# Pairs of gate columns by sums of blocks: seven block products in place of eight, and seven raw buffers

## What is computed

```python
def hybrid_layer(x, norm_w, w_in, ..., w_a_out, w_b_out, w_c_out, w_out, cos, sin, top_k):
    proj = rms_norm_2(x, norm_w) @ w_in
    (qa, ka, va, za, qi, ki, wi, ub, zb, qc, kc, vc, zc, gates) = jnp.split(proj, split_points(), axis=-1)
    ...
    y_a = (dsa_attention(qa, ka, va, qi, ki, wi, top_k) * jax.nn.silu(za)) @ w_a_out
    y_b = (conformer_conv(ub, conv_w, conv_b, cln_w, cln_b) * jax.nn.silu(zb)) @ w_b_out
    y_c = (stick_breaking_attention(qc, kc, vc) * jax.nn.silu(zc)) @ w_c_out
    g = jax.nn.sigmoid(gates).reshape(b, s, N_BRANCH, D_MODEL)
    merged = g[:, :, 0] * y_a + g[:, :, 1] * y_b + g[:, :, 2] * y_c
    return x + merged @ w_out
```

## Time and profile before

| | us |
|---|---|
| median of 3 runs (3021.7 to 3023.07) | 3022.87 |
| span of the profiled execution, first to last instruction | 3020.0 |
| PE busy in it | 3003.1 |
| ACT busy | 2288.5 |
| DVE busy | 2115.0 |

### The profile page before, as it was taken

One profiled execution on the slowest core, in us unless ns is written; L12 is line 12 of the kernel. 1 busy time (PEld: TensorE's weight loads), 2 busy tenths in 40 slices (PEclk: granted clock), 3 DMA queues, 4 the chain that ended last, 5 costly groups with the idle time before them and its releaser, 6 DMA issues.

```text
span 3020.0 us, 37810 instructions
## 1 busy us (share of the span) xinstructions
PE 3003.1 (99%) x13856; PEld 2510.0 (83%) x13856; DVE 2115.0 (70%) x3153; ACT 2288.5 (76%) x4062; POOL 7.7 (0%) x20
## 2 busy tenths in 40 slices
PE   8999999999999999999999999999999999999998
PEld 7888888878888888888888888888888888888887
DVE  6566656767666799999765555658999977555555
ACT  8799988999998677698984446786669999644564
POOL 0000000000000000000000000000000000000000
PEclk9999999999999999999999999999999999999999
DMA  8665665666556665566666666566566656666665
GB/s 307 198 175 167 180 201 174 203 181 178 178 175 199 190 192 176 172 181 181 188 184 194 190 194 196 190 198 192 162 195 180 177 172 196 187 208 192 193 191 165
DMA packets 305801, 570.24 MB, mean 189 GB/s; under 512 B 18352, under 2 KB 45136, under 8 KB 305232
## 3 DMA queue, kind: packets, MB, share of 16 engines
q1 hardware_dynamic: 301728, 557.65, 61.0%
q10 hardware_dynamic: 3040, 6.42, 0.6%
q0 software_dynamic: 848, 3.76, 0.4%
HBM read 565.66 MB, written 2.10 MB: 188 GB/s over the span
## 4 chain that ended last, share of the span: by engine, by line
PE 96%; ACT 3%; issue 0%; DMA 0%; DVE 0%; DVEq 0%; SPq 0%; ACTq 0%
PE gp L113 92%; PE bk L113 4%; ACT G L128 2%; ACT wh L128 1%; PE bk L116 0%; DMA raw<-in_ev_w_mem_kv 0%; ACT tmp L128 0%; ACT nat L128 0%; ACT Yh L128 0%; DVE wl L139 0%; DVE merged L152 0%; DVE X L139 0%; DVE merged L145 0%; DVE gp L146 0%; DVEq L2464 0%
## 5 line engine op out<-in xcount | busy, mean ns | idle before, releaser
L139 DVE TENSOR_TENSOR wl<-raw,wh 128x1024 fp32r<-128x1024 f32 (+2 forms) x1072 | 1281.3, 1201 | 723.7 <-ACT wh L128 719.8
L128 ACT ACTIVATE wh<-raw 128x1024 fp32r<-128x1024 f32 (+2 forms) x1072 | 1111.1, 1044 | 579.7 <-PE gp L113 557.9
L113 PE MATMUL gp<-wh,Hh 128*128 128x512 f32 (+2 forms) x2336 | 905.3, 388 | 0.0
L113 PE MATMUL gp<-wl,Hh 128*128 128x512 f32 (+2 forms) x2336 | 898.3, 385 | 0.0
L113 PE MATMUL gp<-wh,Hl 128*128 128x512 f32 (+2 forms) x2336 | 898.3, 385 | 0.0
L113 PE MATMUL gp<-wh,Yh 128*128 128x512 f32 (+3 forms) x1952 | 758.4, 389 | 8.8 <-DVE wl L139 8.8
L113 PE MATMUL gp<-wh,Yl 128*128 128x512 f32 (+3 forms) x1952 | 753.5, 386 | 0.0
L113 PE MATMUL gp<-wl,Yh 128*128 128x512 f32 (+3 forms) x1952 | 753.4, 386 | 0.0
L113 PEld LDWEIGHTS gp<-wh,Hh 128*128 128x128 f32 x2336 | 438.8, 188 | 87.7 <-issue 2.3
L113 PEld LDWEIGHTS gp<-wh,Hl 128*128 128x128 f32 x2336 | 438.7, 188 | 86.7
L113 PEld LDWEIGHTS gp<-wl,Hh 128*128 128x128 f32 x2336 | 438.9, 188 | 84.9
(11 more groups left out here) (135 smaller groups left out, 1196.7 us busy)
## 6 DMA issues: line engine op xcount, KB each, us to landing
raw<-in_w_in SPq DMA_DIRECT2D x544, 512.0 KB, 3.8
raw<-in_ev_w_in SPq DMA_DIRECT2D x104, 512.0 KB, 3.8
raw<-in_od_w_in SPq DMA_DIRECT2D x80, 512.0 KB, 3.7
raw<-in_w_out SPq DMA_DIRECT2D x64, 512.0 KB, 4.2
raw<-in_ev_w_out SPq DMA_DIRECT2D x40, 512.0 KB, 4.3
raw<-in_od_w_out SPq DMA_DIRECT2D x36, 512.0 KB, 4.0
raw<-in_w_b_out SPq DMA_DIRECT2D x32, 512.0 KB, 4.7
raw<-in_w_a_out SPq DMA_DIRECT2D x32, 512.0 KB, 4.9
```

The source lines that it names most:

```text
L113: return self.e.matmul(out, l, r, start=start, stop=stop)
L128: return self.e.activation(out, in_, func, **kw)
L139: return self.sketch(157 + size(a) * 1.042) if self.e is None else self.e.tensor_tensor(out, a, b, op)
```

## The change

Two neighbouring gate columns n, n + 1 of one branch are computed together, a `Duo`, where `ONLY` says so: branch 1 parts 2 and 3, all of branches 0 and 2, in both layers: ten duos. The two `y` projections follow the two gates. In a duo the eight row block pairs q are laid as two plain fills (role p, one for each column part), except q = 1, 4, 6 (`SEVEN`), where 2 x 2 blocks of the activations (A: token half x row block) and of the weights (B: row block x column part) are multiplied by Winograd's form of Strassen's scheme: seven block products. Two fills a and b are loaded. DVE forms x = (B12 - B11, B12 - B22) (`t_outer`), B22 minus the first of these in place of B12 in b (`t_inner`) and B21 - that in place of B21 in a (`t_last`); x needs a raw buffer but no transfer, y reuses a's second half. `hi` and `lo` then split all four: a, b, x of two row blocks and y of one. The matching sums of the activations are made once per layer and q by `s_sum` (five DVE operations), `s_hi`, `s_lo` into `Sh`, `Sl`, which share memory with a region of G. The products go to eight banks: both `gp` pairs and all four of the `bank` ring, which the duo takes at its first fill. Behind the duo one copy on ACT (`duo_copy`) and `duo_middle`, `duo_outer`, `duo_first`, `duo_mixed`, `duo_end` on DVE (six additions, two of them of 1024 columns) form the four results in the five `tmp` buffers, and tanh reads them from there.

Further: seven raw buffers in place of four; `half` is gone, `merge` adds 1 to the tanh, and the missing factor 0.5 moves into `in_hi` and `in_lo` of the merged values; the second `load_gfin` goes to another region of G and waits for the merged input; the memory for the descriptors of Pool's transfers is set to 4096.

```diff
-RAW = 4
+RAW = 7
 SPLIT = 4
 BY_ACT = (1,)
+SEVEN = (1, 4, 6)
+ONLY = ((1, 2), (0, 0), (0, 2), (2, 0), (2, 2))
...
-        self.raw = [sb(f"raw{i}", [128, 2, 512]) for i in range(RAW)]
+        self.raws = sb("raw", [128, 2 * RAW, 512])
+        self.raw = [self.raws[:, 2 * i:2 * i + 2, :] for i in range(RAW)]
         self.wh = [sb(f"wh{i}", [128, 2, 512], R) for i in range(SPLIT)]
         self.wl = [sb(f"wl{i}", [128, 2, 512], R) for i in range(SPLIT)]
+        with ExitStack() as early:
+            sb("ahead", [128, 1024], F, early)
+            self.Sh, self.Sl = (sb(n, [128, 4 * len(SEVEN), 128], R, early) for n in ("Sh", "Sl"))
...
+                for n in (0, 2):
+                    gates = []
+                    for m in (n, n + 1):
+                        gates.append(gemm(L, "H", 0, W, C["gates"] + 2048 * br + 512 * m, 512, 16, "gate", None, (br, m)))
+                        if (br, n) not in ONLY:
+                            merge[br, m] = (gates[-1], gemm(L, "Y", lo, I[name][l], 512 * m, 512, 8, "y", None, (br, m)))
+                    if (br, n) in ONLY:
+                        duo(*gates)
+                        for m in (n, n + 1):
+                            merge[br, m] = (gates[m - n], gemm(L, "Y", lo, I[name][l], 512 * m, 512, 8, "y", None, (br, m)))
             self.merge.append(merge)
-            self.h_end[L] = gate
+            self.h_end[L] = gates[1]
...
+    def lay_duo(self, d):
+        for q in range(d.a.nk // 2):
+            for role, gm in (zip("abxy", (d.a, d.b, d.b, d.b)) if q in SEVEN else (("p", d.a), ("p", d.b))):
+                f = len(self.fills)
+                self.role[f] = (role, d, q)
+                self.fills.append((gm, q))
+                d.units.append(f)
+                for bank, _, kk, t in self.parts(f):
+                    d.first.setdefault(bank, (f, kk, t))
+                    d.last[bank] = (f, kk, t)
+        d.a.end = d.b.end = f
+
+    def parts(self, f):
+
+        role, d, q = self.role[f]
+        gm, i = self.fills[f][0], 4 * SEVEN.index(q) if q in SEVEN else 0
+        if role == "p":
+            names = ("11", "21") if gm is d.a else ("12", "22")
+            return [(names[t], (kk, t), kk, t) for kk in range(2) for t in range(2)]
+        return {"a": [("1", (0, 0), 0, 0), ("11", (1, 0), 1, 0)], "b": [("6", i + 2, 0, 0), ("12", i + 3, 1, 0)],
+                "x": [("5", i, 0, 0), ("7", i + 1, 1, 0)], "y": [("21", (1, 1), 1, 0)]}[role]
...
+    def place_raw(self):
+
+        self.slot, self.leaves, self.loaded_before = [], [], []
+        holder, n, loaded = [None] * RAW, 0, None
+        for f in range(len(self.fills)):
+            role = self.role[f][0] if f in self.role else None
+            self.loaded_before.append(loaded)
+            if role not in ("x", "y"):
+                loaded = f
+            if role == "y":
+                self.slot.append(self.slot[f - 3])
+                self.leaves.append(None)
+                continue
+            self.slot.append(n % RAW)
+            self.leaves.append(holder[n % RAW])
+            holder[n % RAW] = f + 3 if role == "a" else f
+            n += 1
...
+    def banks_of(self, d):
+        g, h = self.gp[d.a.g % 2], self.gp[d.b.g % 2]
+        return {"1": g[:, 0, :], "11": g[:, 1, :], "6": h[:, 0, :], "22": h[:, 1, :], "12": self.four[:, 0, :],
+                "21": self.four[:, 1, :], "5": self.four[:, 2, :], "7": self.four[:, 3, :]}
...
+            n = gm.duo.n
+            return self.v_duo.at(*(((n, "v1"), (n, "c11")) if gm is gm.duo.a else ((n, "v1"), (n, "c22"))))
...
-        if f < RAW:
+        if f < 4:
             e.behind("load_memt", f)
         else:
-            e.behind("raw", f - 1)
-            e.wait_ge(*P.v_lo.at(f - RAW))
-        if f == RAW:
+            e.behind("raw", P.loaded_before[f])
+        if f == 4:
             e.behind("load_memt", 4)
+        if P.leaves[f] is not None:
+            e.wait_ge(*P.v_lo.at(P.leaves[f]))
...
+        e.wait_ge(*P.v_in.at(*([("m", 1, i) for i in range(0, 16, 2)] if f else [("y", 9, 2)])))
+        e.dma_start(P.gfin[f], g.unsqueeze(0).broadcast_to([128, 2048])).then_inc(*P.s_gfin[f].up("g", 16))
...
+        if f == d.units[0]:
+            for i in range(4):
+                P.bank.take(("duo", d.n, i))
+        e.wait_ge(*P.v_lo.at(f))
+        if f == d.units[0]:
+            e.wait_ge(*P.drained(P.gemms[d.a.g - 2]))
+            for i in range(4):
+                e.wait_ge(*P.bank.free(("duo", d.n, i)))
+        if f == d.units[1]:
+            e.wait_ge(*P.drained(P.gemms[d.b.g - 2]))
+        if role in ("b", "x"):
+            e.wait_ge(*P.v_s.at((P.lhs(gm, 2 * q)[0:2], q)))
+        bk = P.banks_of(d)
+        lh, ll = P.pairs[gm.side][gm.L]
+        for bank, of, kk, t in P.parts(f):
+            if role in ("b", "x"):
+                h, l = P.Sh[:, of, :], P.Sl[:, of, :]
+            else:
+                k, c = 2 * q + of[0], slice(128 * of[1], 128 * of[1] + 128)
+                e.wait_ge(*ready(gm, k))
+                h, l = lh[:, gm.lo + k, c], ll[:, gm.lo + k, c]
+            wh, wl = P.wh[s][:, kk, :], P.wl[s][:, kk, :]
+            e.matmul(bk[bank], h, wh, d.first[bank] == (f, kk, t), False)
+            e.matmul(bk[bank], h, wl, False, False)
+            i = e.matmul(bk[bank], l, wh, False, d.last[bank] == (f, kk, t))
+        i.then_inc(*P.p_mm.up(f))
...
+        role = P.role[f][0] if f in P.role else None
+        if role in ("b", "x", "y"):
+            e.wait_ge(*P.v_tsum.at((f - "abxy".index(role), {"b": 2, "x": 1, "y": 4}[role])))
+        if role not in ("x", "y"):
+            e.wait_ge(*P.raw_loaded(f))
...
+    def t_outer(f):
+
+        a, b, x = (P.slot[f + i] for i in range(3))
+        e.wait_ge(*P.raw_loaded(f))
+        e.wait_ge(*P.raw_loaded(f + 1))
+        if P.leaves[f + 2] is not None:
+            e.wait_ge(*P.v_lo.at(P.leaves[f + 2]))
+        i, j = 2 * a, 2 * b + 1
+        s = slice(i, j + 1, j - i) if i < j else slice(i, j - 1 if j else None, j - i)
+        b12 = P.raw[b][:, 0, :].unsqueeze(1).broadcast_to([128, 2, 512])
+        e.tensor_tensor(P.raw[x], b12, P.raws[:, s, :], ALU.subtract).then_inc(*P.v_tsum.up((f, 1)))
+
+    def t_inner(f):
+        a, b, x = (P.raw[P.slot[f + i]] for i in range(3))
+        e.wait_ge(*P.v_tsum.at((f, 1)))
+        e.tensor_tensor(b[:, 0, :], b[:, 1, :], x[:, 0, :], ALU.subtract).then_inc(*P.v_tsum.up((f, 2)))
+
+    def t_last(f):
+        a, b = (P.raw[P.slot[f + i]] for i in range(2))
+        e.wait_ge(*P.v_tsum.at((f, 2)))
+        e.wait_ge(*P.v_lo.at(f))
+        e.tensor_tensor(a[:, 1, :], a[:, 1, :], b[:, 0, :], ALU.subtract).then_inc(*P.v_tsum.up((f, 4)))
...
+        e.tensor_tensor(a, h, lo[:, at:at + 2, :].bitcast(F), ALU.add).then_inc(*P.v_ssum.up((*key, "a")))
+        e.wait_ge(*P.v_ssum.at((*key, "a")))
+        e.tensor_tensor(s[:, 0, :], a[:, 0, 128:256], a[:, 1, 128:256], ALU.add).then_inc(*P.v_ssum.up((*key, 1)))
+        e.tensor_tensor(s[:, 1, :], a[:, 0, 128:256], a[:, 0, 0:128], ALU.subtract).then_inc(*P.v_ssum.up((*key, 3)))
+        e.wait_ge(*P.v_ssum.at((*key, 1)))
+        e.tensor_tensor(s[:, 2, :], s[:, 0, :], a[:, 0, 0:128], ALU.subtract).then_inc(*P.v_ssum.up((*key, 2)))
+        e.wait_ge(*P.v_ssum.at((*key, 2)))
+        e.tensor_tensor(s[:, 3, :], a[:, 1, 0:128], s[:, 2, :], ALU.subtract).then_inc(*P.v_ssum.up((*key, 4)))
...
+        e.tensor_tensor(T[:, 1, :], P.banks_of(d)["6"], T[:, 0, :], ALU.add).then_inc(*v.up((n, "v1")))
...
+        one = T[:, 1, :].unsqueeze(1).broadcast_to([128, 2, 512])
+        e.tensor_tensor(T[:, 2:4, :], one, P.four[:, 2:4, :], ALU.add).then_inc(*v.up((n, "v2")))
+        e.wait_ge(*v.at((n, "v2")))
+        e.tensor_tensor(T[:, 4, :], T[:, 3, :], P.four[:, 2, :], ALU.add).then_inc(*v.up((n, "c22 begun")))
...
+        e.tensor_tensor(T[:, 0, :], P.banks_of(d)["11"], T[:, 0, :], ALU.add).then_inc(*v.up((n, "c11")))
...
+        e.tensor_tensor(T[:, 2:4, :], T[:, 2:4, :], P.four[:, 0:2, :], ALU.add).then_inc(*v.up((n, "c12")))
...
+        e.tensor_tensor(T[:, 4, :], P.banks_of(d)["22"], T[:, 4, :], ALU.add).then_inc(*v.up((n, "c22")))
...
-    def half(g):
-        b = P.nat.buf(g)
-        e.wait_ge(*P.a_evac.at((g, "end")))
-        e.tensor_scalar(b, b, 0.5, 0.5, ALU.mult, ALU.add).then_inc(*P.v_half.up(g))
...
-            e.tensor_tensor(m, ps[:, :, :], b, ALU.mult).then_inc(*P.v_m.up((g, 0)))
+            e.scalar_tensor_tensor(m, b, 1.0, ps[:, :, :], ALU.add, ALU.mult).then_inc(*P.v_m.up((g, 0)))
...
-        if s.name in ("hi", "lo"):
+        if s.name in ("hi", "lo", "t_outer", "t_inner", "t_last"):
             return 0 if s.args[0] - plan.at_fill <= 3 else 4
-        if s.name == "evac":
+        if s.name == "evac" or s.name[0:3] == "duo":
...
-    nc = _bacc.Bacc("TRN2", target_bir_lowering=False, num_devices=1)
+    nc = _bacc.Bacc("TRN2", target_bir_lowering=False, num_devices=1, dynamic_dma_scratch_size=4096)
```

(52 more changed lines are left out.)

183 lines of the change are left out of this document (148 added, 35 removed).

## The result

| | before | changed |
|---|---|---|
| median of 5 runs, us | 3022.92 | 3002.35 |
| lowest to highest | 3021.7 to 3023.1 | 3001.31 to 3002.67 |
| span of the profiled execution | 3020.0 | 3000.9 |

The ratio is 0.9933, with a 95% interval of 0.9921 to 0.9945: 20.57 us faster. The forecast was 3005.5 us in a range of 3000.5 to 3017, or 3002 to 3010 without rival 1. The kernel before has two runs more here than in the table before the change, so its median moved by 0.05 us.

A forecast was written before the change was run, and what follows sets the result against it. The prediction took PE's own matmul issue to bound the kernel: 3022.87 - 20.4 for removed matmuls + 3 for stalls = 3005.5 us, in a range of 3000.5 to 3017, or 3002 to 3010 as the forecast's own case.

The forecast's parts named there:

- rival 1: In the duos: stalls take 0.2 to 0.6 us from each pair, giving 3014.5 us (3010 to 3016.8); chance 0.16.
- What bounds the kernel: In both merge stages PE is busy every microsecond, so its own issue sets the time, 0.2267 us per matmul.
- 90 matmuls x 0.2267 = 20.4 us: On PE: 30 pairs take 21 matmuls in place of 24, saving 20.4 us in all.
- 2.87 us around the span: Outside the profiled execution: the median of 3022.87 us exceeds the 3020.0 us span by 2.87 us, carried over unchanged.
- Stalls, 0.3 us per duo: PE's waits in the ten duos: 3 us in all, chosen between zero and 19 us.
- hand-run order: DVE's operations from pair 4 to pair 6, timed: they fit with one to three microseconds to spare.
- That needs the seventh raw buffer: DVE running ahead in the pairs needs seven raw buffers, as x occupies one and a stays until y's lo.
- Quarter 2 has 7 us of slack: Before the output projection: quarter 2's flip and 16 moves need 12 us, leaving 7 us of slack.
- half at nothing: Removing half from DVE (24 x 0.694 us) gains nothing, as that engine had idle time; 16.7 us if DVE bound.
- Rival 3: In the pairs DVE becomes the bound, each costing 6.9 us in place of 4.76: 3068 us; chance 0.10.
- Rival 4: Short waits in the duos lower the granted clock and 143 us of pairs would double: 3145 us; chance 0.01.
- The start: At program start, three more transfers of 512 KB go out: value 0, bounds -1 to +2.5 us.

The follow-up runs named there:

- no_duo: The changed kernel with no duo at all, gate columns one by one, all other edits kept; 3022.13 us, ratio 0.9997 to the kernel before.
- raw5: The changed kernel with five raw buffers in place of seven; 3008.31 us, 6.0 us slower than with seven.
- raw6: The changed kernel with six raw buffers in place of seven; 3002.38 us, the same as seven.
- one_pair: The changed kernel with ten duos but only row block pair 4 taking seven products, 10 such pairs in place of 30; 3015.02 us.
- half_back: The changed kernel with the half step back on DVE and the old merge, in_hi and in_lo; 3003.47 us.
- adjacent_pairs: The changed kernel with its seven-product pairs next to each other, 3, 4, 5 in place of 1, 4, 6; 3035.0 us.
- first_gates_b: The changed kernel with two duos more, at each layer's first gates, and the four small banks handed back together at a duo's end; 3029.22 us.
- out_duo: The changed kernel with one duo more, in the first two column parts of the last layer's output projection; 3007.08 us.

## Why the prediction was right, step by step

**What bounds the kernel**: right. Nothing but matmul starts sets the time in the merge stages; no_duo shows that the other edits together are worth zero within 1 us.

**90 matmuls x 0.2267 = 20.4 us**: right. Measured 20.57 between medians. The two profiled executions differ by 19.1 us, and the difference can be followed: the two stretches of duos are 10.1 and 9.8 us shorter, the rest 0.1, and the first duo begins 0.9 us later (1579.59 for 1578.66). The last comes from the start of the program. Both run a first stretch of matmuls 0.43 us apart behind the wait of the start; it is longer in the profiled execution of the changed kernel. The last matmul that starts 0.43 us after the one ahead of it, before and after:

```profile
11.96 0.41 PE L113 MATMUL gp<-wl,Yh 128*128 128x512 f32 x1
```
```profile
14.24 0.52 PE L115 MATMUL gp<-wl,Yh 128*128 128x512 f32 x1
```

They lie 3.2 and 5.7 us behind the first matmul (8.81 and 8.52). The spacing beyond 0.2267 adds up to 1.6 us before and 2.9 after, and the first matmul is 0.3 earlier: 1.0 us. The same excess is 1.8 us in no_duo, 1.9 in raw5, 2.1 in raw6 and 2.7 in one_pair. Among these raw5, raw6 and one_pair differ from the changed kernel only in what comes much later or in a buffer, so I put the difference down to the execution and not to the change; no run settles it. It fits that the profiled execution of the changed kernel has the longest span of its five runs (2999.5 to 3000.9).

**2.87 us around the span**: wrong. Where time and span of a run are both on record, they differ by 1.75 to 1.92 us in all but a few. The 2.87 compared the median with the span of one execution, a short one. The forecast starts from the median, so nothing came of it.

**Stalls, 0.3 us per duo**: the term that was mis-sized. It was 3 us and measured 0.5: the two stretches fall short of 10.2 us each by 0.1 and 0.4. The largest gap is 0.2 us near 2868, and two of 0.1 stand at the second fill of each layer's first duo. That is 2.5 of the 3.1 us by which the forecast missed; the rest is less than the runs scatter. The 3 us was a choice between 0 and 19 that no row gave, so that the number came this near is in part luck, and 3002.35 lies at the very edge of the narrower range of 3002 to 3010. The hand-run order was right in the main. Counted from a of pair 4, which starts at 1600.77 on PE, the rows under raw5 and raw6 give for seven buffers: `lo` of y at 0.9 (foretold 0.98), `t_outer` 1.7 (1.7), `t_inner` 5.2 (4.2), `t_last` 7.1 (8.6), `lo` of b and x done at 10.1 (10.4), `lo` of y at 11.1 (11.1). Only `t_inner` and `t_last` stand elsewhere, 1.0 later and 1.5 earlier than foretold. I had added something for collisions, and as I read it the list planner, which sees each of them, had already arranged them away; no run without it shows that.

**"That needs the seventh raw buffer"**: wrong. raw6 is as fast. Six suffice for the lead; with five it costs 6.0 us. The lead of `t_outer` over b's matmul is what counts: 9.8 us with seven buffers, about 6 with six, and a block without slack with five.

**Quarter 2 has 7 us of slack**: wrong, 1.7 us. I let the flip follow the merge at once and let nothing follow the moves. In the program the first `merge` operation ends at 1886.43, the flip starts 3.8 us later, the 16 moves between `hi`s take 9.0 (1891.67 to 1900.68), and `in_lo` follows only 3.7 after them: 18.7 us in place of 12. half_back shows what stands behind it.

**half at nothing**: right for DVE's time, wrong in that the end of the merge stage was nearer than I had it. The rows named for the new `merge` hold no scalar_tensor_tensor; in the changed kernel it takes 1.22 us at 1024 columns, as assumed (1885.21).

**Rival 3, DVE becomes the bound**: not in this kernel, but real two steps away. Its price was 2.2 us for each pair; adjacent_pairs loses 1.1 us per pair, lower clock included, because in each duo the combinations of the first two pairs are still made ahead, in whole or in part, and PE waits about 2 us in the third alone. **Rival 4, the clock**: cycling through eight banks does not lower it: granted 1.00 in both stretches. The kernel before went round four already, two pairs in turn. The Trainium skill, "TensorE: Matmul & The Clock Gate", section "A second HAM failure mode: psum-queue depth-cycling", tells of an engine that idles for short times between its groups of matmuls while it cycles through banks. A duo has no such pause between its groups, so this case neither confirms nor refutes the page. Where the clock did fall (adjacent_pairs, first_gates_b, out_duo) it fell behind a wait, and the price behind one in adjacent_pairs and out_duo was 1.7 to 2.3 us, not the doubling of whole stages. **The start**: value 0 holds (no_duo).

## What to carry to other kernels

Where PE never waits, a scheme that trades matmuls for elementwise work is worth the removed matmul starts (here to within 1 us of 20), as long as the added work is spread so that its engine can run ahead; count the lead at the narrowest place, not the average load. The same operations in three neighbouring pairs cost 33 us here; with plain pairs between them (1, 4, 6) they cost next to nothing. Look also for what is made only just in time (operand sums, a split quarter) and for its place in the order of the other engines: it decides where the scheme can be extended.

## What had not been expected of the hardware

A wait of about 2 us brought the granted clock to 0.58 for the next 4 us in some cases and not in others of the same length, with the matmuls 0.43 us apart in place of 0.23; behind 4.0 us it was 0.50 for 5 us. At the start of the program the matmuls are 0.43 us apart for 3.2 us in the profile of before and 5.7 us in that of the changed kernel. The clock column reads 1.00 there (this row is of the changed kernel):

```profile
9.00:12.00 3.00, 3.00 (x8) 2.33 (x8) 2.74 (x6) 2.80 (x6) 0.00 (x0) 1.00 1.03 409
```

Eight matmuls in 3 us, where 13 fit. The 1.00 is no measurement: in all twelve kept traces the record of the granted clock has its first entry only where the spacing falls to 0.23 us, to within 0.3 us (at 12.0 us before, at 14.5 in the changed kernel, 11.9 to 14.5 in all), and the column counts time without an entry as full clock. The spacing of 0.43 us is that of the windows that read 0.50. So at the start of a profile the pace is read from the starts of the matmuls, not from this column. Why the stretch ends sooner in one execution than in another stays open.
